# Other row sequences for the branch-output and mixed matmuls of a hybrid decoder layer

## The reference, cut to what matters

```
xn   = rmsnorm(h)
proj = xn @ w_in                       # inputs of three mixers, and three gate groups g_a, g_b, g_c
ya   = fox_attention(...) @ w_a_o      # three branch outputs, 1024 -> 2048 each
yb   = short_conv(...)    @ w_b_o
yc   = gated_linear_attention(...) @ w_c_o
mix  = sigmoid(g_a + b_a) * ya + sigmoid(g_b + b_b) * yb + sigmoid(g_c + b_c) * yc
h    = h + mix @ w_o                   # 2048 -> 2048
u    = causal_conv(rmsnorm(h) @ w_up)
h    = h + (silu(u_gate) * u_up) @ w_down
out  = rmsnorm(h)[meta tokens dropped]
```

## Time and profile before

| | |
|---|---|
| median of 3 runs | 1729.08 us (1728.56 to 1729.19) |
| profiled execution, whole | 1728.02 us |
| its span, first to last instruction | 1726.3 us |
| TensorE busy (matmul) | 1716.1 us, 99% |
| VectorE, ScalarE, GpSimd busy | 65%, 44%, 15% |
| granted TensorE clock, mean | 0.999 |

### The profile page before, as it was taken

The page is one execution under the profiler, slowest core; times in us unless marked ns, Lnnn a source line. Parts: engine busy times, 40 slices in busy tenths (PEclk is TensorE's granted clock), DMA queues, the critical chain, the costliest instruction groups (busy, mean ns, idle before and its releaser), DMA issues.

```text
span 1726.3 us, 34115 instructions
## 1 busy us (share of the span) xinstructions
PE 1716.1 (99%) x13429; PEld 1665.4 (96%) x13429; DVE 1117.4 (65%) x1605; ACT 764.1 (44%) x921; POOL 263.2 (15%) x492
## 2 busy tenths in 40 slices
PE   9999999999999999999999999999999999999998
PEld 8999999999999999999999999999999999888886
DVE  6857767667565554555556687777777777554454
ACT  6635454354354444444444443344444444433443
POOL 4153333630530000000000044321000000000000
PEclk9999999999999999999999999999999999999999
DMA  8566557566565555565655566666555565655554
GB/s 235 171 181 188 168 153 200 174 167 180 159 184 187 179 173 189 175 203 183 194 174 184 187 198 207 205 201 189 185 184 186 187 191 182 224 194 191 189 192 136
DMA packets 310297, 320.63 MB, mean 186 GB/s; under 512 B 17354, under 2 KB 285134, under 8 KB 310094
## 3 DMA queue, kind: packets, MB, share of 16 engines
q1 hardware_dynamic: 296861, 311.01, 57.8%
q0 software_dynamic: 12928, 7.80, 2.1%
q10 hardware_dynamic: 432, 0.79, 0.1%
HBM read 311.10 MB, written 2.11 MB: 181 GB/s over the span
## 4 chain that ended last, share of the span: by engine, by line
PE 99%; DVE 0%; DMA 0%; ACT 0%; SPq 0%; issue 0%; ACTq 0%; DVEq 0%
PE ps L1436 81%; PE ps L1714 5%; PE ps L1713 5%; PE ps L1712 5%; PE ps L1543 1%; DMA xb<-in_x_dram 0%; PE ps L1557 0%; PE ps L1582 0%; PE ps L1572 0%; PE ps L1573 0%; PE ps L1601 0%; PE ps L1602 0%; DVE xl L941 0%; DVE lo L896 0%; PE ps L1474 0%; PE ps L1529 0%
## 5 line engine op out<-in xcount | busy, mean ns | idle before, releaser
L896 DVE TENSOR_TENSOR lo<-raw,hi 128x1024 fp32r<-128x1024 f32 x584 | 710.0, 1230 | 477.7 <-ACT hi L627 475.9
L627 ACT CAST hi<-raw 128x1024 fp32r<-128x1024 f32 x584 | 605.1, 1049 | 654.3 <-PE ps L1436 520.6
L1436 PE MATMUL ps<-xh,hi 128*128 128x260 f32 (+2 forms) x3312 | 530.3, 282 | 0.2 <-DVE xl L941 0.2
L1436 PE MATMUL ps<-xl,hi 128*128 128x260 f32 (+2 forms) x3312 | 527.6, 281 | 0.0
L1436 PE MATMUL ps<-xh,lo 128*128 128x260 f32 (+2 forms) x3312 | 527.3, 281 | 0.0
L1436 PEld LDWEIGHTS ps<-xh,hi 128*128 128x128 f32 x3312 | 450.5, 188 | 1.4 <-issue 0.4
L1436 PEld LDWEIGHTS ps<-xl,hi 128*128 128x128 f32 x3312 | 450.5, 188 | 0.0
L1436 PEld LDWEIGHTS ps<-xh,lo 128*128 128x128 f32 x3312 | 450.2, 188 | 0.0
L610 POOL DMA_DIRECT2D hT<-h2b x128 | 69.4, 551 | 597.6 <-DVE h2b L1286 592.0
L1714 PE MATMUL ps<-lo,act_h 128*128 128x512 f32 x350 | 137.5, 393 | 0.0
L1713 PE MATMUL ps<-hi,act_l 128*128 128x512 f32 x350 | 136.9, 391 | 0.0
(11 more groups left out here) (300 smaller groups left out, 1249.2 us busy)
## 6 DMA issues: line engine op xcount, KB each, us to landing
raw<-in_w_in_dram SPq DMA_DIRECT2D x224, 512.0 KB, 3.5
raw<-in_w_up_dram SPq DMA_DIRECT2D x176, 512.0 KB, 4.7
raw<-in_w_down_dram SPq DMA_DIRECT2D x88, 512.0 KB, 4.5
raw<-in_w_o_dram SPq DMA_DIRECT2D x32, 512.0 KB, 3.3
raw<-in_w_in_dram SPq DMA_DIRECT2D x32, 256.0 KB, 4.0
raw<-in_w_a_o_dram SPq DMA_DIRECT2D x16, 512.0 KB, 4.2
raw<-in_w_b_o_dram SPq DMA_DIRECT2D x16, 512.0 KB, 3.2
raw<-in_w_c_o_dram SPq DMA_DIRECT2D x16, 512.0 KB, 3.2
```

What stands on the lines that cost most here:

```text
L627: nc.scalar.copy(part(ph, i, q, hi_all), raw[:, s, :]).then_inc(hi_ready, 1)
L896: nc.vector.tensor_tensor(part(ph, i, q, lo_all), raw[:, s, :], part(ph, i, q, hi_all).bitcast(F32), ALU.subtract).then_inc(lo_ready, 1)
L1436: ins = nc.tensor.matmul(acc, tiles(weights, s, j, m), moving(j)[side][:, a:], start=first and (kind, at) == (0, 0), stop=last and (kind, ...
```

## The change

Two constants change. The branch outputs get (3, 2, 1, 0). The w_o panels get one sequence for each column group: (3, 0, 1, 2) for the first and (3, 1, 2, 0) for the second. `H2_ROWS` and `ROWS` stay.

```diff
             KINDS = ((hi, 0), (hi, 1), (lo, 0))
             ROWS = (0, 3, 1, 2)
-            BO_ROWS, MIX_ROWS, H2_ROWS = (2, 1, 3, 0), (2, 1, 3, 0), (2, 1, 3, 0)
+            BO_ROWS, MIX_ROWS, H2_ROWS = (3, 2, 1, 0), ((3, 0, 1, 2), (3, 1, 2, 0)), (2, 1, 3, 0)
...
                     use_turns(WO, i, q, st, (lambda k0: lambda j: (mix_h[:, k0 + j, C0:QE], mix_l[:, k0 + j, C0:QE]))(kq * KJ),
-                              NQ, kq == 0, kq == 3, MIX_ROWS)
+                              NQ, kq == 0, kq == 3, MIX_ROWS[st])
```

## The result

The changed kernel takes 1736.16 us (median of 6 runs, 1735.49 to 1738.05), the kernel before 1728.55 us (6 runs, 1728.35 to 1729.19): ratio 1.0044, 95% interval 1.0034 to 1.0054. It is 7.6 us slower, where 1.1 us was forecast; 1736.16 lies above the range of 1727.0 to 1732.6.

The account below looks back on a forecast made before the run. TensorE was taken to bound the kernel, its matmuls back to back. Second w_o group 0.32, first 0.16, branch outputs 0.48 and ring switches 0.16 us gave 1.12 us on 1729.08: 1730.2 us, range 1727.0 to 1732.6.

Parts of the forecast that it names:

- What bounds the kernel: TensorE, busy 99% of the span, waits for nothing in the changed stages; any gain or loss reaches the end undiminished.
- the price of the gate ring at 258 columns: w_o's second column group: (0, 3, 1, 2) entered elsewhere, 117.5 ns, 0.83 over (2, 1, 3, 0); 0.32 us, between 0 and 0.64.
- the prediction's own averages: w_o's first column group and branch outputs: successions at 0, 0.83 and, where unseen, 0.42 ns, averaging 0.42 ns per matmul.
- Pricing by pairs: All new sequences: each succession of one row behind another has its price, 0 or 0.83 ns where the trace shows it.
- Unseen rings: w_o's first column group 0.16 us (-0.64 to +1.28), branch outputs 0.48 us (-1.92 to +3.84), at 0.42 ns per matmul.
- the slower beat: Branch outputs and w_o: new rings run one step (1.67 ns) slower, 1732.4 us, or two, 1735.6 us; chance 0.18.
- Its argument against: Branch outputs and w_o: ring (2, 1, 3, 0) shows one beat only, the same 116.67 ns in both stages.
- Switches: w_o: seven ring changes between its column groups and one into UP, about 0.02 us each; 0.16 us, bounds 0 and 0.3.
- The range: Whole kernel: 1727.0 to 1732.6 us, from one step faster on branch outputs alone to one step slower on all new rings.
- the signs that the prediction named: A new sequence two or more steps off, a new wait in the stream, or changed distances in untouched gate panels or UP.

Follow-up runs that it names:

- e4_swapped: The changed kernel with its three new sequences exchanged: branch outputs (3, 1, 2, 0), w_o's column groups (3, 2, 1, 0) and (3, 0, 1, 2); 1736.82 us.
- e5_map: The changed kernel with untried rings in branch outputs and w_o's first group, (2, 1, 3, 0) in its second, other rings in gate panels; 1737.84 us against 1728.70.
- e3_turned: The changed kernel with branch outputs in (0, 3, 2, 1) instead of (3, 2, 1, 0); 1735.08 us, against 1728.59 for the kernel before.
- e7_lower16: The kernel before, all sequences kept, with the rounded weight panels of all stages up to UP 16 bytes lower; 1761.66 us, beside 1728.70.

## Why the prediction was wrong, point by point

- **What bounds the kernel** held: the chain stays on TensorE, no wait appeared, and a longer distance went to the end undiminished (7.37 us in the chain, 7.6 us in the medians).
- **The step that failed is the price of the gate ring at 258 columns.** The prediction took the 118.33 ns measured at 260 columns, subtracted 0.83 ns for two columns, and so put the ring's successions at 0.83 ns over the old ring, one step at most. The second column group is this ring entered elsewhere: it runs at 121.67 ns, 5.0 ns over (0.32 us forecast; 384 x 5.0 ns = 1.9 us measured). e4_swapped shows the same 121.67 ns in the branch outputs, and e5_map the reverse for the old ring: 116.67 ns at 258 columns, 121.67 at 260. So the distance of a ring at one width does not give that at another. The terms for the other two sequences rest on the same 0.83 ns. As an estimate, the prediction's own averages with 5.0 ns in its place give 2.5 ns for both unseen rings and 1.92 + 0.96 + 2.88 + 0.16 = 5.9 us in place of 1.1, most of the miss.
- **Pricing by pairs** took a succession, such as 0-3, to have a price of its own. It has none that holds even at one width and placement: the gate panels keep their four successions and run at 120.00 ns in the changed kernel and at 118.33 in e3_turned. Whether pair prices measured at the right width would add up is not shown: the six rings of the table's column "as before" use twelve pairs, each in two rings, so any six distances can be split into such prices.
- **Unseen rings** were priced at 0.42 ns. The first column group has 1.67 ns (0.16 us forecast, 0.64 measured), within its bounds. The branch outputs have 3.33 ns (0.48 us forecast; 1,152 x 3.33 ns = 3.84 us, the very end of the bound given). That the bound held is luck in part, since it was the slowest distance seen at 260 columns, and another ring went past it.
- **A term was missing:** the gate panels fell into the slower beat of their ring, 1.1 us. Rows 8 had shown that beat, and the text named a change of the untouched panels as something that would make it wrong, but gave it no price: seven trips x 96 x 1.67 ns = 1.1 us could have been worked out.
- **The rival that came near** is the slower beat, held at 0.18: its two steps give 1735.6 us. Its argument against, that the old ring shows one beat only, said nothing of new rings. Its mechanism, a ring that has two beats and falls into the slower one, is shown for the gate panels alone. The three new rings kept one distance each, in every stage that they were put in (e4_swapped); one of them was also turned, and kept it (e3_turned).
- **Switches**: 0.16 us forecast for eight; there are nine, with the one from the branch outputs into w_o. Behind a switch to the first group of w_o the first panel takes 19 ns more than the settled ones (5 ns in the first trip), behind one to the second group 19 ns less, so they nearly cancel; the term was too small to matter.
- **The range** ended at one step on all; the upper bounds given for the terms, 0.64 + 1.28 + 3.84 + 0.3 = 6.06 us, reach to 1735.1 and still not to 1736.16. What is missing there is the second column group, which went past its bound (1.9 measured, 0.64 given), and the gate panels, which had none. The measured terms, 1.92 + 0.64 + 3.84 + 1.1 = 7.5 us, account for the 7.37 of the chain. Of the signs that the prediction named as showing it wrong two came: two sequences two or more steps off, and a changed distance of the untouched gate panels.

## What to carry to other kernels

Where matmuls stand back to back, read the start-to-start distance panel by panel, not the duration: 1.67 ns on 1,152 matmuls is 1.9 us. The profile's single durations show it unreliably: their mean rose from 279 to 281 to 283 ns for the branch outputs, but stayed at 282 to 283 ns for the matmuls of 260 columns in e7_lower16, although the distance of the gate panels rose by 1.67 ns. A sequence of tiles tuned on the chip belongs to its operand widths and address phases (here, as far as the runs go, modulo 256 bytes); carry it to another width or buffer offset only after measuring, and look also at the stages behind it, whose beat depends on how they are entered. The range for an untested ring should span at least what the six known ones do, 5 ns here.

## What the runs showed of the hardware

- At the upper clock level (granted 1.00, 2.4 GHz) the distances found for 258 columns are 116.67 to 121.67 ns, mostly in steps of 1.67 ns, four 2.4 GHz cycles. Moving the weight panel by 16 bytes changes them by up to 5.0 ns ((0, 1, 2, 3) by 3.3, (0, 3, 1, 2) by -5.0), by 64 bytes with the rows renamed not at all. DN's 512-column matmuls keep 228.89 ns when their weights lie 256 bytes lower.
- One ring at one placement and width can run in two beats (118.33 and 120.00 ns for (0, 3, 1, 2) at 260 columns, before and after), and in the changed kernel the slower one lasts for four panels, until the ring is turned.
- What in the chip makes the weight tile's place matter to the matmul was not seen: the runs show that addresses count, a period that fits and the prices, not the unit in which the two streams meet. That stays open.
